# One weight sum computed, split and read in halves at the three junctions of each feed-forward phase

## The reference, cut to what matters

```python
for i in range(DEPTH):
    x = x + 0.5 * swiglu(rmsnorm(x, ffn1_norm[i]), ffn1_w_gu[i], ffn1_w_down[i])
    x = x + mixer(rmsnorm(x, mix_norm[i]))          # attention, SSD, short convolution, attention
    x = x + 0.5 * swiglu(rmsnorm(x, ffn2_norm[i]), ffn2_w_gu[i], ffn2_w_down[i])

def swiglu(x, w_gu, w_down):
    gate, up = jnp.split(x @ w_gu, 2, axis=-1)
    return (jax.nn.silu(gate) * up) @ w_down
```

## Time and profile before

| | us |
|---|---|
| median of 3 runs | 2016.92 (2016.15 to 2017.0) |
| the profiled execution, its own time | 2016.95 |
| its span in the trace | 2015.2 |
| PE busy | 1987.3 (99%) |
| DVE busy | 1680.8 (83%) |
| ACT busy | 1242.4 (62%) |
| POOL busy | 189.3 (9%) |
| mean granted TensorE clock | 0.999 |

### The profile page before, as it was taken

The page is one execution under the profiler, slowest core; times in us unless marked ns, Lnnn a source line. Parts: engine busy times, 40 slices in busy tenths (PEclk is TensorE's granted clock), DMA queues, the critical chain, the costliest instruction groups (busy, mean ns, idle before and its releaser), DMA issues.

```text
span 2015.2 us, 25299 instructions
## 1 busy us (share of the span) xinstructions
PE 1987.3 (99%) x10203; PEld 1684.0 (84%) x10203; DVE 1680.8 (83%) x1569; ACT 1242.4 (62%) x1317; POOL 189.3 (9%) x181
## 2 busy tenths in 40 slices
PE   7999999999999999999999999999999999999998
PEld 6888998888888889988888878988888888998877
DVE  7997568997999789969987997779988997568996
ACT  6565576665666566646665665446665665576664
POOL 2000001010000014411001010001001000001010
PEclk9999999999999999999999999999999999999999
DMA  9896535996897484368995996758986896535992
GB/s 278 274 268 214 181 105 141 277 258 222 231 270 230 146 271 131 126 230 222 277 272 162 277 253 191 209 186 232 286 257 175 268 267 216 176 105 144 275 261 103
DMA packets 250632, 436.65 MB, mean 217 GB/s; under 512 B 10924, under 2 KB 93188, under 8 KB 250004
## 3 DMA queue, kind: packets, MB, share of 16 engines
q1 hardware_dynamic: 215732, 363.34, 53.1%
q0 software_dynamic: 34496, 71.39, 19.7%
q10 hardware_dynamic: 288, 0.31, 0.0%
HBM read 433.92 MB, written 1.08 MB: 216 GB/s over the span
## 4 chain that ended last, share of the span: by engine, by line
PE 72%; DVE 14%; ACT 7%; issue 4%; DMA 2%; DVEq 0%; ACTq 0%; SPq 0%; POOLq 0%; POOL 0%
PE bank L1620 36%; PE bank L1761 23%; PE bank L1626 7%; DVE w_lo L1126 6%; ACT w_hi L744 6%; PE bank L1795 2%; DVE stage L1264 2%; DVE arena L1487 2%; DVE arena L1264 1%; DMA arena<-in_ffn_w_gu 1%; PE bank L1653 1%; PE bank L1935 1%; PE bank L1966 1%; PE bank L1948 0%; DMA stage<-in_ssd_w_in 0%
## 5 line engine op out<-in xcount | busy, mean ns | idle before, releaser
L1126 DVE TENSOR_TENSOR w_lo<-stage,w_hi 128x2048 fp32r<-128x2048 f32 (+1 forms) x245 | 562.3, 2298 | 85.1 <-ACT w_hi L744 82.5
L744 ACT ACTIVATE w_hi<-stage 128x2048 fp32r<-128x2048 f32 (+1 forms) x245 | 463.0, 1893 | 220.6 <-PE bank L1620 109.8
L1126 DVE TENSOR_TENSOR w_lo<-arena,w_hi 128x2048 fp32r<-128x2048 f32 (+1 forms) x199 | 450.3, 2267 | 81.6 <-ACT w_hi L744 80.0
L744 ACT ACTIVATE w_hi<-arena 128x2048 fp32r<-128x2048 f32 (+1 forms) x199 | 376.7, 1897 | 184.8 <-PE bank L1620 87.3
L1620 PE MATMUL bank<-w_hi,mt_hi 128*128 128x512 f32 x928 | 366.5, 395 | 0.4 <-DVE mt_lo L1373 0.4
L1620 PE MATMUL bank<-w_lo,mt_hi 128*128 128x512 f32 x928 | 361.4, 389 | 0.0
L1620 PE MATMUL bank<-w_hi,mt_lo 128*128 128x512 f32 x928 | 360.8, 390 | 0.0
L1761 PE MATMUL bank<-w_hi,mt_hi 128*128 128x512 f32 x512 | 205.2, 401 | 7.9 <-DVE w_lo L1126 7.8
L1620 PEld LDWEIGHTS bank<-w_hi,mt_lo 128*128 128x128 f32 x928 | 174.2, 188 | 36.9
L1626 PE MATMUL bank<-xt_hi,w_hi 128*128 128x256 f32 x704 | 203.4, 290 | 1.6 <-DVE arena L1487 1.1
L1620 PEld LDWEIGHTS bank<-w_hi,mt_hi 128*128 128x128 f32 x928 | 174.3, 188 | 35.4 <-DVE mt_lo L1373 0.8
(11 more groups left out here) (219 smaller groups left out, 2957.3 us busy)
## 6 DMA issues: line engine op xcount, KB each, us to landing
arena<-in_ffn_w_gu SPq DMA_DIRECT2D x82, 1024.0 KB, 5.9
stage<-in_ffn_w_gu SPq DMA_DIRECT2D x78, 1024.0 KB, 5.3
stage<-in_ffn_w_down SPq DMA_DIRECT2D x100, 512.0 KB, 5.0
arena<-in_ffn_w_down SPq DMA_DIRECT2D x76, 512.0 KB, 5.5
arena<-in_ffn_w_gu POOLq DMA_DIRECT2D x35, 1024.0 KB, 9.0
stage<-in_ffn_w_gu POOLq DMA_DIRECT2D x29, 1024.0 KB, 10.1
arena<-in_ffn_w_gu SPq DMA_DIRECT2D x20, 512.0 KB, 6.9
arena<-in_sb_w_qkv SPq DMA_DIRECT2D x16, 512.0 KB, 4.7
```

The lines of the kernel that those rows point to most:

```text
L744: act.activation(w_hi[q][:, 0:c], stage[s][:, 0:c], ACT.Copy).then_inc(hi_done, 1)
L1126: dve.tensor_tensor(w_lo[q][:, 0:c], stage[s][:, 0:c], w_hi[q][:, 0:c].bitcast(F32), ALU.subtract).then_inc(lo_done, 1)
```

## The change

Only at the 24 junctions, and for one of the POOL reads everywhere:

- DVE makes the A1 weight sum in two instructions of 128 x 1024 (`sum_half` after the first), ACT makes A1's `w_hi` in two (`hi_half`), DVE its `w_lo` in two (`lo_half`).
- DVE's `w_lo` of A1 is moved: it was in the step after the sum, and now stands right behind the sum, ahead of `second_gate`, the sum of A4's partial and the product of the first hidden half.
- PE starts A1 on `lo_half` and waits for the whole block between its second and its third group of three matmuls.
- The adding read for A2 is issued as two reads of 512 KB in all 32 S units. At a junction the first waits for `lo_half` only, the second for A1's `lo_done`; in the other eight units both wait for `lo_done`.

```diff
@@ POOL, weight_sums @@
-                    pool.wait_ge(lo_done, base[p] + FFN_ORDER.index((u, "A1")) + 1)
-                    pool.dma_start(stage[to][:, :].rearrange("p (k c) -> p k c", k=4), b22,
-                                   accum_op=ALU.add).then_inc(a2_in, 16)
+                    f, n = nth("ffn", p), base[p] + FFN_ORDER.index((u, "A1"))
+                    for j in range(2):
+                        if j == 0 and adjacent(u):
+                            pool.wait_ge(lo_half, junctions_to(f, u))
+                        else:
+                            pool.wait_ge(lo_done, n + 1)
+                        pool.dma_start(stage[to][:, HALF[j]].rearrange("p (k c) -> p k c", k=2), b22[:, 2 * j:2 * j + 2, :],
+                                       accum_op=ALU.add).then_inc(a2_in, 16)
@@ ACT, split @@
+                if name == "A1" and adjacent(u):
+                    act.wait_ge(block_used, n - SPLIT_SLOTS + 1)
+                    act.wait_ge(sum_half, junctions_to(nth("ffn", p), u))
+                    act.activation(w_hi[q][:, HALF[0]], stage[s][:, HALF[0]], ACT.Copy).then_inc(hi_half, 1)
+                    act.wait_ge(w_summed, len(SUM_STEP) * sums + SUM_STEP[name])
+                    act.activation(w_hi[q][:, HALF[1]], stage[s][:, HALF[1]], ACT.Copy).then_inc(hi_done, 1)
+                    return
@@ DVE, ffn @@
+                def weight_sum_by_halves(u):
+                    w = lambda b: stage[home[p, u, b][0]]
+                    dve.wait_ge(lo_done, b0 + FFN_ORDER.index((u, "B11")) + 1)
+                    dve.wait_ge(stage_in[home[p, u, "B12"][0]], home[p, u, "B12"][1])
+                    dve.tensor_tensor(w("B11")[:, HALF[0]], w("B12")[:, HALF[0]], w("B11")[:, HALF[0]],
+                                      ALU.add).then_inc(sum_half, 1)
+                    dve.tensor_tensor(w("B11")[:, HALF[1]], w("B12")[:, HALF[1]], w("B11")[:, HALF[1]],
+                                      ALU.add).then_inc(w_summed, 1)
+                def split_by_halves(u, n):
+                    s, q = slot_of[n], n % SPLIT_SLOTS
+                    dve.wait_ge(hi_half, junctions_to(f, u))
+                    dve.tensor_tensor(w_lo[q][:, HALF[0]], stage[s][:, HALF[0]], w_hi[q][:, HALF[0]].bitcast(F32),
+                                      ALU.subtract).then_inc(lo_half, 1)
+                    dve.wait_ge(hi_done, n + 1)
+                    dve.tensor_tensor(w_lo[q][:, HALF[1]], stage[s][:, HALF[1]], w_hi[q][:, HALF[1]].bitcast(F32),
+                                      ALU.subtract).then_inc(lo_done, 1)
...
-                    if i + 2 <= len(FFN_ORDER) and (i == 0 or FFN_ORDER[i - 1] != (N_UNITS - 1, "A2")):
+                    if i + 2 < len(FFN_ORDER) and FFN_ORDER[i + 2][1] == "A1" and adjacent(FFN_ORDER[i + 2][0]):
+                        pass
+                    elif i + 2 <= len(FFN_ORDER) and (i == 0 or FFN_ORDER[i - 1] != (N_UNITS - 1, "A2")):
                         split(b0 + i + 2)
...
                         if name == "B11" and adjacent(u):
-                            weight_sum(u, "A1")
+                            weight_sum_by_halves(u)
+                            split_by_halves(u, b0 + i + 3)
                             second_gate(u - 1)
@@ PE, ffn @@
-                def product(n, out_, x_, start, stop):
+                def product(n, out_, x_, start, stop, whole_from=None):
                     for k in range(4):
+                        if k == whole_from:
+                            block_in(n)
...
-                    if n > 0:
+                    if name == "A1" and adjacent(u):
+                        pe.wait_ge(lo_half, junctions_to(f, u))
+                    elif n > 0:
                         block_in(n)
```

More of the change, by code:

```diff
@@ L98, in ffn_order, with junctions_to @@
     return order + waiting + [(u, f"D{j}") for j in range(down_parts(u))], turned
+def junctions_to(f, u):
+    return f * sum(adjacent(v) for v in range(len(UNITS))) + sum(adjacent(v) for v in range(u + 1))
+HALF = (slice(0, 1024), slice(1024, 2048))
 FFN_ORDER, TURNED_AFTER = ffn_order()
@@ L431, in build_trunk @@
         first_hi, first_lo = sem("first_hi"), sem("first_lo")
+        sum_half, hi_half, lo_half = sem("sum_half"), sem("hi_half"), sem("lo_half")
         xt_ps = sem("xt_ps")
@@ L736, in split @@
                 elif name == "A2":
-                    act.wait_ge(a2_in, 16 * (sums + 1))
+                    act.wait_ge(a2_in, 32 * (sums + 1))
                 elif name == "A3":
@@ L1259, in weight_sum @@
                         if BY_DMA:
-                            dve.wait_ge(a2_in, 16 * (sums_before(f, u) + 1))
+                            dve.wait_ge(a2_in, 32 * (sums_before(f, u) + 1))
                         else:
@@ L1822, in ffn @@
                         pe.wait_ge(xs_lo_done, 4 * (f + 1))
-                        product(n, bank[5], x_sum_part(0), True, True)
+                        product(n, bank[5], x_sum_part(0), True, True, 2 if adjacent(u) else None)
                     elif name == "B22":
```

## The result

| | before | changed |
|---|---|---|
| median, us (lowest to highest, 4 runs each) | 2016.96 (2016.15 to 2017.28) | 2038.2 (2034.98 to 2038.7) |
| ratio, with its 95% interval | 1 | 1.0101 (1.0089 to 1.0114) |
| span of the profiled execution | 2015.2 | 2036.4 |
| granted TensorE clock | 0.999 | 0.999 |

What follows compares the result with a forecast made beforehand. PE, busy 99%, was taken to bound the kernel. At 24 junctions 0.39 us each, 9.4 us, less 0.3 for the reads, is 9.1 us more than 2016.92: 2026.0 us, range 2015 to 2033, about 8 in 10.

Steps and rivals of the forecast that it cites:

- What bounds the kernel, and the loss at A1: PE, busy 99%, waits for DVE's `w_lo` at A1: 0.59 us lost a junction, 24 of them 14.2 us.
- The price of a half: A 1024-wide piece of A1's sum or split: 1.22 us on DVE, starts 1.14 apart, and 1.05 us on ACT.
- The order, `second_gate` and B22: `second_gate` pushed back, ACT idle some 1.9 us before the second silu, B22 0.38 us later than now.
- Behind B22: D0's load some 0.12 us late, swallowed but for 0 to 0.05 us; the 0.4 us stay and don't grow.
- The two reads: POOL, 9% busy, issues 32 more DMAs; A2's block lands up to 2 us earlier, 0.3 us gained in all.
- Rival 3: A2's read lands 2.0 us later in eight unit 1s: 8.5 us, 2034.5; chance 0.05, shared with junctions losing over 0.7.
- The sum: Over the whole kernel: 24 x 0.39 = 9.4 us at junctions, less 0.3 for the reads, 9.1 us slower.
- The signs named in advance: Profile signs at A1, DVE's halves, `second_gate`, ACT and bank 5's copy, plus a PE gap of about 0.85 us before B22.

Runs made afterwards that it cites:

- read_whole: The changed kernel with A2's adding read in one 1 MB piece again, issued on A1's whole low half: 2030.63 us, ratio 1.0063.
- gate_first: The changed kernel with `second_gate` moved ahead of A1's two low halves, A2's read still in two: 2020.82 us, ratio 1.0015.
- reads_alone: The kernel before, with only A2's read issued as two of 512 KB, both behind A1's `lo_done`: 2028.62 us, ratio 1.0053.
- bytes_less_two: The changed kernel with 2 MB of A2's reads left out over all four units of the first feed-forward (output wrong): 2038.61 us.
- gate_first_whole: The changed kernel with `second_gate` ahead of A1's low halves and A2's read in one piece again: 2008.2 us, ratio 0.9955.
- halves_in_place: The changed kernel with A1's low halves at their old place behind three 512-wide steps, A2's read whole: 2010.3 us, ratio 0.9965.

## Why the prediction was right in kind and wrong in size

The step that failed is the one on the two reads (below): it was put at a gain of 0.3 us and cost 7.1. The kernel with the junctions as changed and the read whole (read_whole) takes 2030.63 us, which lies in the range; the changed kernel's 2038.2 do not. A smaller part was mis-sized, D0 behind B22.

*What bounds the kernel, and the loss at A1.* Right. The wait ahead of A1 is gone and the 0.59 us with it; undisturbed junctions of gate_first, in which nothing else is late, gain 0.64.

*The price of a half.* Right: 1.22 and 1.04 to 1.06 us, with starts 1.14 apart on DVE. The interpolation between two rows of the trace was enough.

*The order, `second_gate` and B22.* Right, and the best part of it: the step from one waiting place (A1) to the next (B22) was found from two margins of 0.74 and 0.9 us. Weight sum to second silu: 5.35 us forecast, 5.40 measured in the later junction. B22's load: 0.38 late forecast, 0.42 measured, 24 times 0.04 or 1 us too little. That `w_lo` and the copy would be done at nearly the same time was right too. In the first junction ACT's high half starts 0.40 us behind the half sum instead of the 0.09 of later ones, and the loss is 0.87 instead of 0.55.

*Behind B22.* Mis-sized. "The 0.2 us between load and matmul swallow" the lateness of D0 "but for a few hundredths; 0 to 0.05": it was 0.13 us, 3 us in all. D0's load is late enough that its first matmul starts 0.04 late, and then the second follows 0.31 us behind the first (81.44, 81.75) instead of 0.23. It is the same slow restart that the prediction had itself counted as 0.10 at A1; it was not charged to D0.

*The two reads.* This is the step that failed: "POOL issues 32 more DMAs, at 9% busy", and a gain of 0.3 us. It was 7.1 us of loss, 9.7 in reads_alone. A share of busy time said that POOL has time; it doesn't say that POOL is never held. The 0.3 us were had (the 24 gaps ahead of B11 are 4.8 us instead of 5.1), but the earlier landing was mis-sized as well: A2's block is in 14.6 us behind A3's issue against 15.3 before (medians of the junctions), 0.7 us earlier and not up to 2. Rival 3 had the read landing late, with the right culprit, the wrong place (unit 1) and the wrong mechanism. It gave the last byte 2.0 us in unit 1; in reads_alone it comes 0.3 us later there, 15.1 us behind A3's issue against 14.8, and 0.4 us later at a junction (medians). By the fit that the Trainium skill ("DMA: Bandwidth & Descriptors", section "Anatomy of one DMA — SWDGE (gpsimd) path") gives for a POOL-issued DMA, a fixed part of about 2.0 us, the estimate was at most 2.0 us; the traces have those 0.3 to 0.4 us, and the holds, which no size would give. Rival 3's 8.5 us of price are near the measured 7.1 to 9.7 by chance. And it was priced as a rival to the forecast, though nothing kept both from happening together: 13.2 and 7.1 add.

*The sum.* Term by term: junctions 9.4 forecast, 13.2 measured (1 at B22, 3 at D0); reads -0.3 forecast, 7.1 measured; the opening 0 forecast, 1.0 measured and unexplained. The range ended at 2033 because it allowed up to 0.7 us a junction (wide enough for the 0.55 measured) and nothing at all for the reads. No row showed a 512 KB read by POOL, and that was said; the range should have held a cost for it on top of the junctions' cost.

*The signs named in advance.* All six were there, if not all in size: no wait ahead of A1; 1.14 us from start to start; `second_gate` 2.79 us later against the sum than before in the first junction (2.42 forecast, and 2.48 in the later junction, which lacks the extra 0.3 us of the first); ACT idle 2.08 (1.9); the copy of bank 5 with no idle time ahead; the gap ahead of B22, 1.20 us at its load in the later junction (0.85).

## What to carry to other kernels

Taking a wait away by moving work forward in an in-order queue moves the wait to whoever needed the work that was passed: look for the next place where the released engine meets its suppliers, and add up both margins there (here 0.59 us were won and about 1.0 lost). Halving a long step so that its consumer may begin on the first half was worth 6.6 us with the order left alone and 8.7 us with the low halves moved ahead of two short steps but not of `second_gate`; it needed no move. And a change of how many pieces a transfer is issued in is a change of its own, to be measured alone and not bundled with one of order.

## What the hardware showed that was not expected

- POOL's time to issue an adding read goes more by reads than by bytes: 1.28 us for 1 MB, 1.2 us for 512 KB, 0.87 us for 256 KB (bytes_less_two); two halves take 2.4.
- POOL can be held 3.1 to 6.9 us between two reads. The hold ends 0.25 us after an earlier read has landed, in all 17 cases, and its place follows the bytes issued (moved by the 2 MB left out, twice) and not the instructions or the number of reads.
- A read that adds, issued 2.42, 2.87, 4.07 or 4.28 us behind another one (read_whole, gate_first_whole, halves_in_place, before), took 12.2, 12.7, 11.6 or 11.0 us to land (medians of the 24 junctions): issued up to 1.9 us earlier, it was in at most 0.6 us earlier.
